# The expert weights of a mixture-of-experts stage in one contiguous piece per partition

## The chip, the cores and the metric

One core of a Trainium2 chip runs the whole program as one launch. The metric is the device time of that launch in microseconds (us). Before the change its median over three runs is 3550.05 us (3540.06 to 3554.87).

## The reference

The program computes two blocks on 512 tokens of 1024 features. The first is a convolution module and a retention module, the second is two layers of windowed attention with local mixers, each followed by a layer of routed experts. All is float32. The change touches only the routed experts and what feeds them. Cut to that:

```
# second block, per layer l (0: 512 + 256 context tokens, 1: 512 tokens)
hx = x * (1 + sc2) + sh2                       # modulated rows, 1024 features
y  = hier_moe(hx, w_rg, b_rg, w_re, b_re, w1, w3, w2)
x  = layer_norm(ALPHA * x + g2 * y, ln2_g, ln2_b)

def hier_moe(h, ...):
    g_logit = h @ w_rg + b_rg                  # 4 groups, the best one is taken
    e_logit = (h @ w_re + b_re) of that group  # 8 experts each, the best two
    gates   = p_group * softmax(best two)
    # per expert e, for its rows xb:
    ys = (silu(xb @ w1[e]) * (xb @ w3[e])) @ w2[e]    # w1, w3: 1024x512; w2: 512x1024
    return sum over a token's two experts of gate * ys
```

There are 32 experts in each of the two layers. The three matrices of one expert hold 2 MB each.

## The kernel before

**Stages.** The first block takes the span up to about 1350 us, then follow attention and mixers of layer 0, the experts of layer 0 (about 1680 to 2340 us), attention and mixers of layer 1, and the experts of layer 1 (about 2820 to 3500 us).

**What feeds the experts.** `modulated` on DVE (line 1415) writes `x * (1 + scale)` of 128 tokens to `b_hx`, and `add_shift` on POOL (line 1828) adds the shift in place. Both run for four sets of rows, q = 0 to 3: the even ones feed the attention of layer q/2, the odd ones the experts. For an odd q, ACT's DMA queue (line 787) writes the rows to `moe_in` in DRAM, and PE transposes them (line 968) and multiplies them with the router weights `b_wr` (line 1104). Feature k*128+p of a row stands on partition p as piece k, in the rows and in the router weights alike.

**The experts.** The rows of each expert are padded to blocks of 64. The 32 experts are shared out to two streams s = 0, 1 (the even and the odd ones), and the engines go round the streams: block i of stream 0, block i of stream 1, block i+1 of stream 0, and so on (`rounds`, line 366). Each stream has its own slots for w1, w3 and w2, its own rows and its own PSUM banks. A block is done like this:

- POOL gathers its 64 rows from `moe_in` with an indirect DMA (line 1888). Rows that are only padding are out of bounds and are left out.
- PE transposes them (line 1132), DVE copies them (1726), PE makes the two products with w1 and w3 (1145, 32 matmuls).
- ACT takes SiLU (805), DVE multiplies gate, SiLU and the other product into `m_h` (1752).
- PE transposes `m_h` (1156), DVE copies (1734), PE multiplies with w2 (1168, 16 matmuls), ACT (812) and DVE (1742) copy the result.
- POOL scatters the 64 rows to `moe_out` with an indirect DMA (line 1904).

PE's order in one step (`expert_step`, line 1173) is: products of block i, transposes of the hidden rows of block i-1, transposes of the rows of block i+1, outputs of block i-1; then the same for the other stream. POOL's order (`move_step`, line 1909) is: gather for block i+1, scatter of block i-1. So the scatter of one stream stands just ahead of the gather of the other in POOL's queue.

**The loads.** SP loads w1 and w3 of block i+1 when the products of block i are done, and w2 of block i when the outputs of block i-1 are done (`load_step`, line 565). `cond=new` leaves a load out where the block has the same expert as the one before it. In the tile `m_w` partition p holds, for each k, a row of 512 floats (w1, w3; k = 0 to 7) or of 1024 floats (w2; k = 0 to 3), and the row is row k*128+p of the matrix in DRAM:

```
ws = [a[k][l].rearrange("e (k p) n -> p (e k) n", p=P) for k in ("w1", "w3", "w2")]
sp.dma_start(m_w[s][j], ws[j][:, bass.ds(e * kk[j], kk[j]), :], cond=new)
```

A load therefore fills each partition from 8 separate stretches of 2 KB of DRAM (w1, w3) or from 4 of 4 KB (w2). All weights go through SP's DMA queue, gathers and scatters through POOL's queue; both share the core's 16 DMA engines.

Of the kernel before, what the change touches and what calls it, by code (L numbers as in the profile page):

```python
# [14 lines left out]
ALU = mybir.AluOpType  # L15
# [5 lines left out]
P = 128  # L21
D = 1024
KD = D // P
S = 512
C = 256
TX, TC = S // P, C // P
# [18 lines left out]
SB = 64  # L45
# [57 lines left out]
def build(nc, a, out, stop=None):  # L103
    ctx = ExitStack()
    with ctx:
# [9 lines left out]
        def mem(at, n, parts=P):  # L115
            return arena[0:parts, at:at + n]
# [45 lines left out]
        def ada_cols(v, g):  # L162
# [75 lines left out]
        m_si = [mem(W0 + 16800 + 8 * s, 1, SB).bitcast(I32) for s in range(2)]  # L238
        m_w = [[mem(RING + CHUNK * (3 * s + j), CHUNK).rearrange("p (k c) -> p k c", k=k)
                for j, k in enumerate((KD, KD, KE))] for s in range(2)]  # L240

# [189 lines left out]
        def _(sp):  # L431
# [85 lines left out]
            for l in range(LAYERS):  # L517
# [11 lines left out]
                for who in ((0, 1) if l == 0 else (0,)):  # L529
                    for i_, j in enumerate((2, 4, 3)):  # L530
                        mod_row(l, who, j, 3 * who + i_)
                sp.dma_start(b_wr, a["w_router"][l].rearrange("(k p) n -> p k n", p=P)).then_inc(sem("wr"), 16)
                sp.dma_start(mem(o_r, E * E), a["lower"]).then_inc(sem("wr"), 16)

                ws = [a[k][l].rearrange("e (k p) n -> p (e k) n", p=P) for k in ("w1", "w3", "w2")]
                kk = (KD, KD, KE)
                sp.wait_ge(sem("ob_mm"), past("ob_mm", l) + 2 * nt)
                for j, what in enumerate(("w1", "w3", "w2")):
                    sp.dma_start(m_w[0][j], ws[j][:, 0:kk[j], :]).then_inc(moe(l, 0, what), 16)

# [8 lines left out]
                for j, what in enumerate(("w1", "w3", "w2")):  # L549
                    sp.dma_start(m_w[1][j], ws[j][:, kk[j]:2 * kk[j], :]).then_inc(moe(l, 1, what), 16)  # L550
                sp.wait_ge(sem("meta"), past("meta", l) + 1)
                last = last_blocks(sp, l)

                def weights(s, j, what, e, new):

                    sp.dma_start(m_w[s][j], ws[j][:, bass.ds(e * kk[j], kk[j]), :], cond=new)\  # L556
                        .then_inc(moe(l, s, what), 16)
# [634 lines left out]
        def _(dve):  # L1192
# [170 lines left out]
            def finish_rows(q, tiles, first, mod_q, sc, free=None):  # L1363
# [22 lines left out]
                def mod_next(i_):  # L1386
                    dve.wait_ge(sem("row_x"), past_rows(q) + i_ + 1)
                    if mod_q % 2 == 0:
                        dve.wait_ge(sem("mod_in"), past("mod_in", mod_q // 2) + 64)
                    if free and tiles[i_] >= TX:  # L1390
                        free()
                    modulated(tiles[i_], sc)

# [20 lines left out]

            def modulated(t, sc):

                dve.scalar_tensor_tensor(out=b_hx[:, t, :], in0=b_mod[sc[t >= TX]], scalar=1.0, in1=xr[:, t, :],  # L1417
                                         op0=ALU.add, op1=ALU.mult).then_inc(sem("hx_scaled"), 1)
# [11 lines left out]
            for t in mod_order(0):  # L1430
                if t < TX:
                    dve.wait_ge(sem("fin_x"), t + 1)
                modulated(t, (3, 5))
            for i_ in range(T):
                mod_copy(0, i_)
            for l in range(LAYERS):
# [307 lines left out]
                def gate_step(s, i, early):  # L1744

                    if early >= 1:
# [4 lines left out]
                    dve.wait_ge(moe(l, s, "silu"), count(l, s, "silu", i + 1))  # L1751
                    dve.scalar_tensor_tensor(out=m_h[s], in0=m_sg[s], scalar=gate, in1=bank(4 * s)[0:SB],
                                             op0=ALU.mult, op1=ALU.mult).then_inc(moe(l, s, "hidden"), 1)
# [28 lines left out]
        def _(pool):  # L1782
# [45 lines left out]
            def add_shift(q, i_, sh):  # L1828
                t = mod_order(q)[i_]
                pool.wait_ge(sem("hx_scaled"), past("hx_in", q) + i_ + 1)  # L1830
                pool.tensor_tensor(b_hx[:, t, :], b_hx[:, t, :], b_mod[sh[t >= TX]], ALU.add)\  # L1831
                    .then_inc(sem("hx_in"), 1)
# [151 lines left out]
```

## Time and profile before

| | |
|---|---|
| median of 3 runs | 3550.05 us (3540.06 to 3554.87) |
| profiled execution, its time | 3556.9 us |
| its span | 3555.1 us |
| PE busy | 2875.6 us, 81% |
| DVE, ACT, POOL busy | 1172.8, 446.7, 416.5 us |
| mean granted clock | 0.88 |
| HBM read | 737.51 MB |

In the page a matmul's line is that of the kernel, DMA share is the mean busy share of the 16 DMA engines in a stretch, and GB/s what they moved. A granted clock of 1 is 2.4 GHz, 0.5 is 1.2 GHz.

### The profile page before, as it was taken

The page shows a single profiled execution, that of the slowest core. Times are in us where ns is not written, and L with a number is a line of the kernel's source. Part 1 is how long each engine was busy: PE and PEld are TensorE (multiplying, and loading weights), DVE is VectorE, ACT ScalarE, POOL GpSimd, SP SyncE. Part 2 cuts the span into 40 slices and gives each one's busy share as a digit, 9 for nine tenths or more (in the row PEclk, how much of TensorE's full clock was granted, in tenths as well). Part 3 has the DMA queues.
Part 4 walks back from the last instruction along what each step waited for, and adds up shares of the span by engine and source line. Part 5 has one row for each costly group of instructions (what it writes and reads, how often), then busy time and mean ns, then how long its engine had stood idle before and what let it go on. Part 6 is the DMA issues. An engine that isn't in the chain of part 4 may idle for free.

```text
span 3555.1 us, 33336 instructions
## 1 busy us (share of the span) xinstructions
PE 2875.6 (81%) x11308; PEld 1305.6 (37%) x11308; DVE 1172.8 (33%) x2041; ACT 446.7 (13%) x845; POOL 416.5 (12%) x488
## 2 busy tenths in 40 slices
PE   7999889999996996794888877818868488898872
PEld 3444334444443554443333222205434323333320
DVE  4899822300112214445111111164254411111114
ACT  2111131001100013400000000000141000000000
POOL 0110030000002000014111111122000311111111
PEclk9999999999998996795989898858879588998786
DMA  6666411221111210015768999751100597469992
GB/s 205 196 201 201 154 41 69 80 86 71 47 66 41 74 42 0 1 43 208 261 249 322 386 386 361 267 193 39 48 1 26 197 381 291 152 218 391 391 338 115
DMA packets 272120, 607.97 MB, mean 171 GB/s; under 512 B 18548, under 2 KB 43253, under 8 KB 270640
## 3 DMA queue, kind: packets, MB, share of 16 engines
q1 hardware_dynamic: 255216, 580.30, 45.1%
q0 software_dynamic: 15392, 21.47, 2.1%
q10 hardware_dynamic: 1440, 5.24, 0.4%
q8 instruction: 45, 0.74, 0.1%
q14 instruction: 27, 0.22, 0.0%
HBM read 737.51 MB, written 29.34 MB: 216 GB/s over the span
## 4 chain that ended last, share of the span: by engine, by line
PE 61%; DMA 13%; DVE 10%; issue 7%; ACT 3%; POOL 3%; SPq 2%; POOLq 1%; DVEq 0%; ACTq 0%
DMA arena<-moe_in,arena 10%; PE psum L1168 10%; PE psum L863 9%; PE psum L910 9%; PE psum L997 8%; PE psum L884 6%; PE psum L1089 4%; PE psum L1145 3%; SPq L556 2%; PE psum L1063 2%; PE psum L1132 2%; ACT arena L752 2%; PE psum L848 1%; DVE arena L1551 1%; DMA arena<-in_w 1%
## 5 line engine op out<-in xcount | busy, mean ns | idle before, releaser
L1145 PE MATMUL psum<-arena 128*64 128x512 f32 x2656 | 599.3, 604 | 35.7 <-DMA arena<-in_w 20.0
L1168 PE MATMUL psum<-arena 128*64 128x512 f32 x1328 | 404.6, 766 | 3.0 <-DVE arena L1734 2.6
L1145 PEld LDWEIGHTS psum<-arena 128*64 128x64 f32 x2656 | 196.3, 140 | 423.2 <-issue 422.8
L863 PE MATMUL psum<-arena 128*128 128x512 f32 x768 | 345.3, 603 | 2.9 <-ACT arena L625 2.9
L910 PE MATMUL psum<-arena 128*128 128x512 f32 x768 | 329.9, 592 | 0.8 <-ACT arena L617 0.8
L1244 DVE SCALAR_TENSOR_TENSOR arena<-arena 128x512 f32<-128x512 f32 x464 | 308.8, 747 | 0.0
L997 PE MATMUL psum<-arena 128*128 128x512 f32 (+1 forms) x800 | 284.5, 518 | 11.1 <-DMA arena<-in_w_in 10.2
L884 PE MATMUL psum<-arena 128*128 128x512 f32 x512 | 223.7, 600 | 11.1 <-POOL arena L1816 10.4
L1734 DVE COPY arena<-psum 128x256 f32<-128x256 f32 x83 | 35.3, 425 | 589.6 <-PE psum L1156 589.6
L1132 PE MATMUL psum<-arena 64*128 64x64 f32 x696 | 72.4, 259 | 179.0 <-DMA arena<-moe_in,arena 179.0
L910 PEld LDWEIGHTS psum<-arena 128*128 128x128 f32 x768 | 145.8, 190 | 184.2 <-issue 183.2
L863 PEld LDWEIGHTS psum<-arena 128*128 128x128 f32 x768 | 143.0, 191 | 174.9 <-issue 174.9
L997 PEld LDWEIGHTS psum<-arena 128*128 128x128 f32 x800 | 152.6, 191 | 142.1 <-issue 133.5
L1168 PEld LDWEIGHTS psum<-arena 128*64 128x64 f32 x1328 | 113.6, 174 | 230.2 <-issue 224.2
L1904 POOL DMA_INDIRECT moe_out<-arena x79 | 74.0, 937 | 1000.6 <-DVE arena L1742 1000.6
L1826 POOL TENSOR_TENSOR arena<-arena 128x1024 f32<-128x1024 f32 x20 | 58.6, 2931 | 858.7 <-DVE arena L1384 858.7
L1742 DVE COPY arena<-psum 64x512 f32<-64x512 f32 x83 | 57.5, 693 | 299.6 <-PE psum L1168 299.6
L884 PEld LDWEIGHTS psum<-arena 128*128 128x128 f32 x512 | 98.5, 193 | 135.9 <-issue 134.7
L1089 PE MATMUL psum<-arena 128*128 128x512 f32 x320 | 137.9, 593 | 1.7 <-ACT arena L769 1.7
L1831 POOL TENSOR_TENSOR arena<-arena 128x1024 f32<-128x1024 f32 x22 | 65.6, 2996 | 623.7 <-DVE arena L1417 623.7
L1726 DVE COPY arena<-psum 128x512 f32<-128x512 f32 x87 | 60.2, 692 | 236.3 <-PE psum L1132 235.6
L1132 PEld LDWEIGHTS psum<-arena 64*128 64x128 f32 x696 | 61.4, 167 | 190.1 <-issue 190.0
(253 smaller groups left out, 2352.2 us busy)
## 6 DMA issues: line engine op xcount, KB each, us to landing
arena<-in_w SPq DMA_DIRECT2D x257, 2048.0 KB
arena<-in_w_ada SPq DMA_DIRECT2D x48, 1024.0 KB, 5.2
arena<-in_conv_w_in SPq DMA_DIRECT2D x24, 1024.0 KB
arena<-in_ret_w_in SPq DMA_DIRECT2D x12, 2048.0 KB, 7.9
arena<-in_w_in SPq DMA_DIRECT2D x8, 2048.0 KB, 18.7
arena<-mod_rows SPq DMA_DIRECT2D x20, 512.0 KB, 8.5
arena<-moe_out SPq DMA_DIRECT2D x10, 1024.0 KB, 9.2
arena<-in_conv_w_out SPq DMA_DIRECT2D x4, 2048.0 KB, 10.2
```

The lines of the kernel that those rows point to most:

```text
L556: sp.dma_start(m_w[s][j], ws[j][:, bass.ds(e * kk[j], kk[j]), :], cond=new)\
L752: act.activation(sb, sb, ACT.Exp, bias=stats[:, o + 4 + hh:o + 5 + hh], accum_out=stats[:, o + 12 + hh:o + 13 + hh]).then_inc(sem("at_e"), 1)
L863: m = pe.matmul(bank(b + c), w[:, k, c * P:(c + 1) * P], c_hT[:, k, :], start=(k == 0), stop=(k == KD - 1))
L884: m = pe.matmul(bank(2 * t + hf), mem(y + S * k + P * t, P), slot_rows(n)[:, k % 4, hf * CW:(hf + 1) * CW], start=(k == 0), stop=(k == KI ...
L910: m = pe.matmul(bank(4 * (n % 2) + j), l_, r_, start=(k == 0), stop=(k == KD - 1))
L997: m = pe.matmul(o, l_, r_, start=(k == 0), stop=(k == KD - 1))
L1089: m = pe.matmul(bank(2 * (t % 4) + hf), y[:, t * P:(t + 1) * P], slot_rows(base + 4 + k // 4)[:, k % 4, hf * CW:(hf + 1) * CW], start=(k = ...
L1132: m = pe.transpose(bank(4 * s + 1, SB, SB * k), m_xs[s][:, k * P:(k + 1) * P], ident[0:SB, 0:SB])
L1145: m = pe.matmul(bank(4 * s)[part], m_xsT[s][:, k, :], m_w[s][j][:, k, :], start=(k == 0), stop=(k == KD - 1))
L1168: m = pe.matmul(bank(4 * s + 3)[SB * hf:SB * hf + SB], m_hT[s][:, k, :], m_w[s][2][:, k, hf * CW:(hf + 1) * CW], start=(k == 0), stop=(k = ...
L1244: ins = dve.scalar_tensor_tensor(out=acc, in0=u, scalar=w[:, j:j + 1], in1=acc, op0=ALU.mult, op1=ALU.add)
L1904: pool.indirect_dma_start(out=moe_out[l], in_=m_y[s], in_offset=None, out_offset=bass.IndirectOffsetOnAxis(m_si[s], 0), bounds_check=2 * n ...
```

## The change

The three weight matrices are read so that partition p takes rows p*8 to p*8+7 (w1, w3) or p*4 to p*4+3 (w2) of the matrix. In DRAM these rows are neighbours, so each partition's share is one stretch of 16 KB. The slot in SBUF keeps its layout: piece k of partition p is now feature p*8+k (w1, w3) or hidden feature p*4+k (w2).

The other operand of each product has to follow. PE still transposes columns k*128 to k*128+127 of a row, so feature p*8+k has to stand in column k*128+p: `modulated` and `add_shift` write the rows in that order where they feed the experts (odd q), and the product with gate writes `m_h` likewise with 4 in place of 8. The router weights are read in the same feature order, which makes one stretch of 1152 bytes per partition of eight of 144 bytes.

No engine gets or loses a compute instruction, and their order stays. SP issues the same DMAs in the same order with other shapes. On DVE and POOL the odd-q instructions get the shape 128x128x8 in place of 128x1024 with a step of 512 bytes between neighbours in SBUF; for even q both sides stay contiguous.

```diff
-        m_w = [[mem(RING + CHUNK * (3 * s + j), CHUNK).rearrange("p (k c) -> p k c", k=k)
-                for j, k in enumerate((KD, KD, KE))] for s in range(2)]
+        m_slot = [[mem(RING + CHUNK * (3 * s + j), CHUNK) for j in range(3)] for s in range(2)]
+        m_w = [[m_slot[s][j].rearrange("p (k c) -> p k c", k=k) for j, k in enumerate((KD, KD, KE))]
+               for s in range(2)]
+        def feature_order(v):
+            return v.rearrange("p (f k) -> p f k", k=KD)
+        def hx_out(q, t):
+            return b_hx[:, t, :].rearrange("p (f k) -> p f k" if q % 2 == 0 else "p (k f) -> p f k", k=KD)
...
-                sp.dma_start(b_wr, a["w_router"][l].rearrange("(k p) n -> p k n", p=P)).then_inc(sem("wr"), 16)
+                sp.dma_start(b_wr, a["w_router"][l].rearrange("(p k) n -> p k n", p=P)).then_inc(sem("wr"), 16)
...
-                ws = [a[k][l].rearrange("e (k p) n -> p (e k) n", p=P) for k in ("w1", "w3", "w2")]
+                ws = [a[k][l].rearrange("e (p k) n -> p e (k n)", p=P) for k in ("w1", "w3", "w2")]
...
-                    sp.dma_start(m_w[s][j], ws[j][:, bass.ds(e * kk[j], kk[j]), :], cond=new)\
+                    sp.dma_start(m_slot[s][j].unsqueeze(1), ws[j][:, bass.ds(e, 1), :], cond=new)\
                         .then_inc(moe(l, s, what), 16)
...
-                dve.scalar_tensor_tensor(out=b_hx[:, t, :], in0=b_mod[sc[t >= TX]], scalar=1.0, in1=xr[:, t, :],
+                dve.scalar_tensor_tensor(out=hx_out(q, t), in0=feature_order(b_mod[sc[t >= TX]]), scalar=1.0,
+                                         in1=feature_order(xr[:, t, :]),
                                          op0=ALU.add, op1=ALU.mult).then_inc(sem("hx_scaled"), 1)
...
-                    dve.scalar_tensor_tensor(out=m_h[s], in0=m_sg[s], scalar=gate, in1=bank(4 * s)[0:SB],
+                    dve.scalar_tensor_tensor(out=m_h[s].rearrange("t (k f) -> t f k", k=KE),
+                                             in0=m_sg[s].rearrange("t (f k) -> t f k", k=KE), scalar=gate,
+                                             in1=bank(4 * s)[0:SB].rearrange("t (f k) -> t f k", k=KE),
                                              op0=ALU.mult, op1=ALU.mult).then_inc(moe(l, s, "hidden"), 1)
...
-                pool.tensor_tensor(b_hx[:, t, :], b_hx[:, t, :], b_mod[sh[t >= TX]], ALU.add)\
+                pool.tensor_tensor(hx_out(q, t), hx_out(q, t), feature_order(b_mod[sh[t >= TX]]), ALU.add)\
                     .then_inc(sem("hx_in"), 1)
```

## Rows read from the trace of the kernel before

**Rows 1.** The page: span in 40 slices, PE and DMA, then GB/s.

```profile
PE   7999889999996996794888877818868488898872
DMA  6666411221111210015768999751100597469992
GB/s 205 196 201 201 154 41 69 80 86 71 47 66 41 74 42 0 1 43 208 261 249 322 386 386 361 267 193 39 48 1 26 197 381 291 152 218 391 391 338 115
```

**Rows 2.** Waits in 1650 to 2500 us, then 2820 to 3500: us, times, longest.

```profile
PE psum L1132 <- DMA arena<-moe_in,arena: 90.8, 32, 7.1
PE psum L1145 <- DMA arena<-in_w: 13.5, 4, 5.2
...
PE psum L1132 <- DMA arena<-moe_in,arena: 88.1, 37, 5.3
PE psum L1145 <- DMA arena<-in_w: 6.5, 1, 6.5
```

**Rows 3.** The source view of line 1145: PE idle until the weights landed, us, times.

```profile
  DMA arena<-in_w: 20.0, 5
```

**Rows 4.** Timeline near 3400 us: start, us, engine line, tiles, [idle before].

```profile
3393.88 7.03 PE L1145 MATMUL psum<-arena 128*64 128x512 f32 x32
...
3395.78 0.93 POOL L1904 DMA_INDIRECT moe_out<-arena  x1 [13.86 <-DVE arena L1742]
...
3397.75 0.96 POOL L1888 DMA_INDIRECT arena<-moe_in,arena  x1 [0.85 <-POOL arena L1885]
...
3404.80 1.08 PE L1132 MATMUL psum<-arena 64*128 64x64 f32 x8 [3.51 <-DMA arena<-moe_in,arena]
3405.82 5.70 PE L1168 MATMUL psum<-arena 128*64 128x512 f32 x16
...
3411.35 0.59 PE L1145 MATMUL psum<-arena 128*64 128x512 f32 x2
```

**Rows 5.** Timeline near 3095 us, and the next block.

```profile
3091.09 7.03 PE L1145 MATMUL psum<-arena 128*64 128x512 f32 x32
...
3094.95 0.95 POOL L1888 DMA_INDIRECT arena<-moe_in,arena  x1 [0.85 <-POOL arena L1885]
...
3098.68 0.68 PE L1132 MATMUL psum<-arena 64*128 64x64 f32 x8 [0.17 <-DMA arena<-moe_in,arena]
3099.29 3.65 PE L1168 MATMUL psum<-arena 128*64 128x512 f32 x16
...
3102.78 0.60 PE L1145 MATMUL psum<-arena 128*64 128x512 f32 x2
```

**Rows 6.** Windows: us, busy by engine, clock, DMA share, GB/s.

```profile
425.00:437.00 12.00, 0.00 (x0) 0.00 (x0) 10.42 (x16) 0.00 (x0) 1.47 (x2) 0.57 1.01 411
2346.00:2358.00 12.00, 0.00 (x0) 0.00 (x0) 10.90 (x16) 0.35 (x2) 0.00 (x0) 0.50 1.01 425
2364.00:2376.00 12.00, 0.00 (x0) 0.00 (x0) 11.72 (x12) 0.20 (x1) 6.18 (x2) 0.50 1.05 391
```

**Rows 7.** The page's DMA issues: KB each, us from issue to landing.

```profile
arena<-in_ret_w_in SPq DMA_DIRECT2D x12, 2048.0 KB, 7.9
```

**Rows 8.** Timeline near 1850 us, after a block that loads nothing.

```profile
1836.71 1.88 PE L1145 MATMUL psum<-arena 128*64 128x512 f32 x8
...
1843.64 7.04 PE L1145 MATMUL psum<-arena 128*64 128x512 f32 x32
...
1845.53 0.93 POOL L1904 DMA_INDIRECT moe_out<-arena  x1 [9.01 <-DVE arena L1742]
...
1847.61 0.96 POOL L1888 DMA_INDIRECT arena<-moe_in,arena  x1 [0.95 <-POOL arena L1885]
...
1854.10 1.09 PE L1132 MATMUL psum<-arena 64*128 64x64 f32 x8 [3.03 <-DMA arena<-moe_in,arena]
```

**Rows 9.** Groups by line and shape: DVE and POOL, busy us, mean ns.

```profile
L1752 DVE SCALAR_TENSOR_TENSOR arena<-arena,psum 64x512 f32<-64x512 f32 x83 | 60.6, 730 | 0.0
L1831 POOL TENSOR_TENSOR arena<-arena 128x1024 f32<-128x1024 f32 x22 | 65.6, 2996 | 623.7 <-DVE arena L1417 623.7
```

**Rows 10.** Timeline of the rows for the experts of layer 1.

```profile
2772.77 5.57 POOL L1831 TENSOR_TENSOR arena<-arena 128x1024 f32<-128x1024 f32 x2 [1.16 <-DVE arena L1417]
...
2776.08 1.97 PE L968 MATMUL psum<-arena 128*128 128x128 f32 x8 [2.71 <-POOL arena L1831]
```

More of the change, by code:

```diff
@@ L531, in _ @@
                         mod_row(l, who, j, 3 * who + i_)
-                sp.dma_start(b_wr, a["w_router"][l].rearrange("(k p) n -> p k n", p=P)).then_inc(sem("wr"), 16)
+                sp.dma_start(b_wr, a["w_router"][l].rearrange("(p k) n -> p k n", p=P)).then_inc(sem("wr"), 16)
                 sp.dma_start(mem(o_r, E * E), a["lower"]).then_inc(sem("wr"), 16)
-                ws = [a[k][l].rearrange("e (k p) n -> p (e k) n", p=P) for k in ("w1", "w3", "w2")]
-                kk = (KD, KD, KE)
+                ws = [a[k][l].rearrange("e (p k) n -> p e (k n)", p=P) for k in ("w1", "w3", "w2")]
                 sp.wait_ge(sem("ob_mm"), past("ob_mm", l) + 2 * nt)
                 for j, what in enumerate(("w1", "w3", "w2")):
-                    sp.dma_start(m_w[0][j], ws[j][:, 0:kk[j], :]).then_inc(moe(l, 0, what), 16)
+                    sp.dma_start(m_slot[0][j], ws[j][:, 0, :]).then_inc(moe(l, 0, what), 16)
                 sp.wait_ge(sem("hx_in"), past("hx_in", 2 * l + 1) + nt)
@@ L549, in _ @@
                 for j, what in enumerate(("w1", "w3", "w2")):
-                    sp.dma_start(m_w[1][j], ws[j][:, kk[j]:2 * kk[j], :]).then_inc(moe(l, 1, what), 16)
+                    sp.dma_start(m_slot[1][j], ws[j][:, 1, :]).then_inc(moe(l, 1, what), 16)
                 sp.wait_ge(sem("meta"), past("meta", l) + 1)
@@ L1391, in mod_next @@
                         free()
-                    modulated(tiles[i_], sc)
+                    modulated(mod_q, tiles[i_], sc)
                 dve.wait_ge(sem("row_w"), 32 * (q + 1))
@@ L1413, in finish_rows, with modulated @@
                     mod_copy(mod_q, i_)
-            def modulated(t, sc):
-                dve.scalar_tensor_tensor(out=b_hx[:, t, :], in0=b_mod[sc[t >= TX]], scalar=1.0, in1=xr[:, t, :],
+            def modulated(q, t, sc):
+                dve.scalar_tensor_tensor(out=hx_out(q, t), in0=feature_order(b_mod[sc[t >= TX]]), scalar=1.0,
+                                         in1=feature_order(xr[:, t, :]),
                                          op0=ALU.add, op1=ALU.mult).then_inc(sem("hx_scaled"), 1)
@@ L1432, in _ @@
                     dve.wait_ge(sem("fin_x"), t + 1)
-                modulated(t, (3, 5))
+                modulated(0, t, (3, 5))
             for i_ in range(T):
```

## The prediction

> **What bounds the kernel now.** I read the page's 40 slices first, then the waits of PE in the two stages of the experts, then the timeline of single blocks, and last short windows in which only one kind of transfer runs.
>
> In the slices [rows 1] DMA counts only where the experts run. Slices are 89 us. Slices 19 to 26 and 32 to 39 are the experts' stages, and in five of them the rate is 381 to 391 GB/s with a DMA share of 9 tenths or more (1955 to 2133 us, 2844 to 2933 us, 3200 to 3377 us). PE is busy 7 or 8 tenths there. Neither engine is plainly the bound, so the waits must tell.
>
> PE waits for the weights themselves hardly at all: 13.5 us in layer 0 and 6.5 us in layer 1 [rows 2], five waits in all, 20.0 us [rows 3]. It waits for the gathered rows 32 times in layer 0 (90.8 us) and 37 times in layer 1 (88.1 us) [rows 2]. So the transfer that holds PE is the small gather of 64 rows on POOL's queue, not the 6 MB of weights.
>
> Two blocks show what the gather costs. Near 3400 us, with the DMA engines full, the gather is issued at 3397.75 and PE's transposes start at 3404.80, 7.05 us later, after PE has idled 3.51 us; from one set of products to the next it is 3411.35 - 3393.88 = 17.47 us [rows 4]. Near 3095 us the same gather takes 3098.68 - 3094.95 = 3.73 us, PE idles 0.17 us, and the block lasts 3102.78 - 3091.09 = 11.69 us [rows 5]. Of the 5.78 us between them 3.34 are the idle time; another 2.05 are in the 16 output matmuls, 5.70 us against 3.65 [rows 4, 5], which run partly at the lower clock after PE has idled. So each block is a ring: outputs, DVE copy, scatter, gather, transposes, outputs of the other stream. The weights' transfers lengthen the ring through the gather.
>
> **The change part by part.**
>
> *Weights in 16 KB pieces.* The trace has no 16 KB piece of this queue, so I take its cost from three full windows [rows 6]. The 2 KB pieces of in_w_in go at 391 GB/s, the 4 KB pieces of conv_w_out at 411, the 8 KB pieces of moe_out at 425. One of 16 engines thus takes 2048 B / 24.4 GB/s = 84 ns, 159 ns and 308 ns for a piece. From 4 to 8 KB that is 74.4 ns for each further 2 KB, so 16 KB should take 308 + 4 x 74.4 = 606 ns, an estimate. A load of 128 pieces is 8 for each engine: 4.85 us, against 64 x 84 ns = 5.36 us (w1, w3) and 32 x 159 ns = 5.10 us (w2). An expert comes to 14.55 us after 15.82, 1.27 us or 8% less. For 64 experts that is 81 us of DMA time. The bounds: none of it is worth anything where the ring sets the pace, all of it where DMA does.
>
> Where does it meet PE? First in the five direct waits [rows 3], of which I let half go: -10 us (0 to -20). Second in the ring. In a 17.5 us block w1 and w3 are issued when the products end (3400.9) and the next scatter follows at about 3413.2, 12.3 us later. The page gives 7.9 us from issue to landing for 2 MB in 2 KB pieces [rows 7], 2.5 us above the 5.36 of transfer; 2 x 4.85 + 2.5 = 12.2 us are then through. Only w2, issued when the outputs end, stands before scatter and gather. It ends 5.10 - 4.85 = 0.25 us sooner. For 64 loading blocks that is -16 us. The ends: 0 if the gather passes w2 anyway, and -1.27 us for each block, -81 us, if DMA sets the pace; between them I stay near the ring, since the waits [rows 2] put 179 us on the gather and 20 on the weights.
>
> *What the long pieces do to the small ones.* Scatter and gather bring 64 rows each, 4 rows and one completion count for each engine: 10 small packets. Behind a queue of 2 KB pieces and one of 4 KB pieces the gather takes about the same, 6.49 us [rows 8] and 7.05 us [rows 4]. If every small packet lets one weight piece pass, it waits 10 x 84 ns = 0.8 us today and 10 x 606 ns = 6.1 us then, 5.2 us more, provided at least 10 pieces are queued for each engine. In the ordinary block they aren't: w2 has 8 pieces, some of them done. After a block that loads nothing they are: near 1845 us the outputs follow the products so soon that the scatter goes out at 1845.53, 7 us after w1 and w3 could be issued (products end at 1836.71 + 1.88 = 1838.59 [rows 8]); of their 12.2 us 5.2 are left, some 8 pieces, and the 8 of w2 stand behind them. There are 83 blocks (instances of line 1752 [rows 9]) and 64 experts, so 19 blocks load nothing; about ten of them are followed by one that does. With 1.3 us each, a quarter of the full price because the queue that delays the gather is empty afterwards and the next gather goes free, this is +13 us (0 to +52).
>
> The Trainium skill says in "DMA: Bandwidth & Descriptors", section on queues, rings and completion order, that a DMA engine goes round its queues at packet granularity and drains a whole packet before it switches. That the two [rows 4, 8] are nearly equal neither supports nor excludes it, since both kinds of piece are short; by that rule the 5.2 us are real wherever the queue is deep. This is the rule that speaks against the change, and the second rival below is built on the same mechanism.
>
> *Strided writes.* DVE's product with the gate takes 730 ns [rows 9]. It writes each element 512 B from the last; the trace has no such write. Even doubled it is done in 1.5 us beside the outputs' 3.65 us or more, with DVE free until these end. Cost 0; without the cover 0.73 us x 83 = 61 us. The router's rows are written by DVE and then added to by POOL, 10 times each. In layer 0 POOL keeps ahead of PE, which is busy with the previous tile's router products. In layer 1 PE waits 2.71 us for POOL's shift, of which two take 5.57 us [rows 10]. Bounds: 0, or twice as long, +5.6 us; I take the middle, +3 us, as DVE's write goes with it.
>
> "GPSIMD Engine Reference" of the Trainium skill, in its performance pitfalls, puts an SBUF read with a step over 8 bytes at 2.9 cycles an element in place of 1.9. By this the two instructions would cost 2.8 us more; no row here has such a step.
>
> *Router weights.* 128 longer pieces in place of 1024 short ones, loaded while PE is at the output projection. Cost 0.
>
> **The sum.** -10 - 16 + 13 + 3 = -10 us on the profiled execution's 3556.9 us: 3546.9. The median stands 7 us below that execution, so I predict 3540 us.
>
> **The rivals.**
>
> *Faster: DMA sets the pace.* For it speak the five slices at 381 to 391 GB/s and the five waits for weights. Against it speak 179 us of waits for rows beside 20 for weights. If half of the 81 us come back, with a share of blocks in which PE's idle time gets so short that the outputs run in 3.65 us and not 5.70 (say 5 x 2 us), it is -50: 3500 us. All of it and more such blocks would be 3460.
>
> *Slower: the gather behind long pieces.* One mechanism, at the gather of a loading block, from the point where 10 pieces (6 us of transfer) are queued for each engine. Its full price is 5.2 us a block. Against it: the longer the gather waits, the further the queue empties, so it can't hit every block. If it takes 1.3 us on the mean in 64 blocks instead of in 10, it is +83 - 13 = +70 beside the sum: 3610 us. At a third of that, 3565.
>
> *It doesn't do what it says.* The pieces are split on the way, or DRAM gives no more for 16 KB than for 4 KB. Then only the strided writes are left: 3550 to 3556 us. Against it speaks the growth up to 8 KB [rows 6].
>
> **How the numbers follow.** A run of this kernel can tell about 0.5%, 17.8 us, from no change, so faster means below 3532 and slower above 3568. My forecast has 0.32, the rival that nothing happens 0.06; both lie within the bound: same 0.38. DMA as the bound has 0.36: faster 0.36. The gather behind long pieces has 0.26: slower 0.26. The likeliest case alone is 3525 to 3560. The range for 8 in 10 takes in most of both rivals: 3490 to 3600.
>
> **What will show it.** (1) Full windows of the experts' stage read 425 to 432 GB/s; at 391 the first term is wrong. (2) The waits of line 1132 for the gathered rows: near 165 us in all for my forecast, below 120 for the first rival, above 230 for the second; and a loading block after an idle one has its transposes 8 us or more after the gather is issued. (3) Line 1145's waits for weights fall to about 10 us. (4) The gate product stays under 1.5 us and nobody waits for it; line 1831's rows for the experts take 2.8 to 5.6 us. (5) Everything before 1500 us is unchanged. The forecast fails if the gathers' waits move by more than 50 us either way.

## The result, and the profile after the change

| | before | after |
|---|---|---|
| median, same chip | 3552.46 us (3540.06 to 3568.31, 20 runs) | 3566.94 us (3551.12 to 3576.74, 20 runs) |
| ratio of the times | 1 | 1.0032, 95% interval 1.0017 to 1.0048 |
| profiled execution, span | 3555.1 us | 3559.2 us |
| DMA packets | 272120 | 131064 |

The change makes the kernel slower by 0.32%, 11 us. The forecast was 3540 us, 10 us faster than the 3550.05 us it started from. The time lies in the range, the direction is wrong.

A single execution of either kernel lies up to 16 us from its median, and the two profiled ones are 4.1 us apart. So sizes below come from ratios, and the profiles show where waits are; each profile is one execution. All lines of PE and ACT are 8 higher after the change: 1132 is now 1140, 1145 is 1153, 1156 is 1164, 1168 is 1176. DVE's 1752 is 1761, POOL's 1831 is 1842, the gather is 1899, the scatter 1915.

The page after the change: 40 slices, then q1 (the weights' queue), then PE's groups with busy time, mean ns and idle time before them.

```profile
DMA  6566411221111200015668998651100497459982
GB/s 210 190 201 201 154 48 62 94 71 71 47 66 52 80 25 0 1 43 208 263 265 326 386 393 336 261 193 39 48 1 26 185 374 274 182 200 392 388 360 118
...
q1 hardware_dynamic: 114160, 580.30, 42.6%
...
L1153 PE MATMUL psum<-arena 128*64 128x512 f32 x2656 | 592.9, 599 | 12.9 <-DMA arena<-in_w 7.4
L1176 PE MATMUL psum<-arena 128*64 128x512 f32 x1328 | 387.8, 738 | 2.2 <-DVE arena L1743 1.8
...
L1140 PE MATMUL psum<-arena 64*128 64x64 f32 x696 | 72.7, 259 | 229.5 <-DMA arena<-moe_in,arena 229.5
```

The same page of before has q1 at 45.1% of the span. 45.1% of 3555.1 us is 1603 us and 42.6% of 3559.2 us is 1516 us: the weights take 87 us less of DMA time. The pieces themselves are as fast as forecast: in the packet records of the trace after the change a piece of 16384 bytes takes 611 ns (median; 606 was estimated), and there are 24576 of them, 128 for each of 192 loads, so none is split. In the trace before, pieces of 2048 and 4096 bytes take 84 to 86 and 159 to 160 ns.

None of the 87 us is left at the end. The five slices with 381 to 391 GB/s [rows 1] read 374 to 393 now; DMA stands idle in the gained time. That shows in a window over the loop of layer 0: us, busy by engine, clock, DMA share, GB/s. First before, then after.

```profile
1700.00:2330.00 630.00, 505.86 (x2334) 184.87 (x2332) 96.42 (x158) 45.70 (x77) 87.57 (x152) 0.88 0.88 318
```

```profile
1700.00:2330.00 630.00, 495.54 (x2318) 180.16 (x2314) 109.83 (x156) 45.67 (x77) 87.39 (x151) 0.88 0.81 318
```

The DMA share falls from 0.88 to 0.81 at the same 318 GB/s. PE's waits after the change, in 1650 to 2500 us and then in 2820 to 3500 us, answer to [rows 2]:

```profile
PE psum L1140 <- DMA arena<-moe_in,arena: 129.0, 36, 7.6
...
PE psum L1140 <- DMA arena<-moe_in,arena: 100.5, 38, 7.1
PE psum L1153 <- DMA arena<-in_w: 7.4, 1, 7.4
```

The waits for weights fall from 20.0 to 7.4 us, those for the gathered rows rise from 179.0 [rows 2, 90.8 + 88.1] to 229.5. The timeline after the change near 2015 us shows two blocks in a row, to be held against [rows 4]:

```profile
2001.80 7.04 PE L1153 MATMUL psum<-arena 128*64 128x512 f32 x32
2003.68 0.94 POOL L1915 DMA_INDIRECT moe_out<-arena  x1 [13.87 <-DVE arena L1751]
...
2005.78 0.97 POOL L1899 DMA_INDIRECT arena<-moe_in,arena  x1 [0.95 <-POOL arena L1896]
...
2015.88 1.09 PE L1140 MATMUL psum<-arena 64*128 64x64 f32 x8 [6.65 <-DMA arena<-moe_in,arena]
2016.89 5.81 PE L1176 MATMUL psum<-arena 128*64 128x512 f32 x16
2022.54 7.03 PE L1153 MATMUL psum<-arena 128*64 128x512 f32 x32
...
2026.31 0.96 POOL L1899 DMA_INDIRECT arena<-moe_in,arena  x1 [0.85 <-POOL arena L1896]
...
2031.28 0.69 PE L1140 MATMUL psum<-arena 64*128 64x64 f32 x8 [1.32 <-DMA arena<-moe_in,arena]
2031.89 3.65 PE L1176 MATMUL psum<-arena 128*64 128x512 f32 x16
```

From the first gather's issue to the transposes it takes 2015.88 - 2005.78 = 10.10 us, from the second's 4.97 us. Before it was 7.05 us in [rows 4], and 7.22, 6.41 and 6.17 us in the three blocks from 2004 to 2044 us. Counting transposes that start after 4.5 us or more of idle time in the whole timeline gives 3 before (17.8 us in all) and 23 after (135.1 us).

The DMA issues of a window with full queues, 1960 to 2050 us, show how long the small transfers take. The last number is the median of us from issue to landing. First before, then after.

```profile
moe_out<-arena POOLq DMA_INDIRECT x5, 5.6
arena<-moe_in,arena POOLq DMA_INDIRECT x5, 6.0
```

```profile
moe_out<-arena POOLq DMA_INDIRECT x5, 8.8
arena<-moe_in,arena POOLq DMA_INDIRECT x5, 7.2
```

The scatter, first of the two in POOL's queue, takes 3.2 us longer (2.6 in the window from 3200 to 3370 us: 8.2 after 5.6). Its 5 packets for each engine at 606 - 84 to 606 - 159 ns, the prediction's piece times, are 2.2 to 2.6 us.

The typical gather is no slower, only some are much slower. Over all 87 gathers the median from issue to landing goes from 5.9 to 5.4 us and the mean from 5.5 to 5.9; those over 8 us go from 1 to 21.

The packet records also say how many pieces pass. Take a scatter and the gather behind it: 160 small packets, 10 for each engine. From the first to the last of them, 0.34 pieces of 16 KB start for each small packet at the median of layer 0 (0.18 in layer 1), and 0.93 (0.96) or more in the highest tenth of such pairs. That stretch lasts 4.2 us on the mean (3.5 in layer 1), and 7.3 (6.1) or more in its longest tenth; before it was 3.5 (3.2) and 4.7 (3.8). So one piece for each small packet is what the worst blocks come near, not the rule. With short pieces the median is 2.1 (2.5), more than one for one.

### The profile page after: what moved, and what is told of

The parts are those of the page before. It is cut to its first block, busy times and chain, and to the rows that moved or that the text cites. A ratio compares the mean times of both kernels' runs of the same rounds, so it can differ in the third digit from the quotient of the medians.

```text
span 3559.2 us, 33336 instructions
## 1 busy us (share of the span) xinstructions
PE 2851.0 (80%) x11308; PEld 1297.9 (36%) x11308; DVE 1210.4 (34%) x2041; ACT 446.7 (13%) x845; POOL 426.1 (12%) x488
## 2 busy tenths in 40 slices
DMA packets 131064, 607.97 MB, mean 171 GB/s; under 512 B 16500, under 2 KB 41461, under 8 KB 105008
## 3 DMA queue, kind: packets, MB, share of 16 engines
q1 hardware_dynamic: 114160, 580.30, 42.6%
## 4 chain that ended last, share of the span: by engine, by line
PE 61%; DMA 14%; DVE 10%; issue 7%; POOL 3%; ACT 3%; POOLq 1%; SPq 0%; DVEq 0%; ACTq 0%
DMA arena<-moe_in,arena 13%; PE psum L1176 11%; PE psum L871 9%; PE psum L918 9%; PE psum L1005 8%; PE psum L892 6%; PE psum L1097 4%; PE psum L1153 3%; PE psum L1140 2%; ACT arena L760 2%; PE psum L1071 2%; DVE arena L1751 1%; PE psum L856 1%; DVE arena L1560 1%; PE psum L939 1%
## 5 line engine op out<-in xcount | busy, mean ns | idle before, releaser
L1153 PE MATMUL psum<-arena 128*64 128x512 f32 x2656 | 592.9, 599 | 12.9 <-DMA arena<-in_w 7.4
L1176 PE MATMUL psum<-arena 128*64 128x512 f32 x1328 | 387.8, 738 | 2.2 <-DVE arena L1743 1.8
L1153 PEld LDWEIGHTS psum<-arena 128*64 128x64 f32 x2656 | 192.7, 139 | 396.3 <-issue 395.9
L1140 PE MATMUL psum<-arena 64*128 64x64 f32 x696 | 72.7, 259 | 229.5 <-DMA arena<-moe_in,arena 229.5
L1176 PEld LDWEIGHTS psum<-arena 128*64 128x64 f32 x1328 | 109.2, 169 | 216.8 <-issue 210.5
L1837 POOL TENSOR_TENSOR arena<-arena 128x1024 f32<-128x1024 f32 x20 | 62.1, 3107 | 852.2 <-DVE arena L1392 852.2
L1842 POOL TENSOR_TENSOR arena<-arena 128x1024 f32<-128x1024 f32 x22 | 71.7, 3274 | 626.2 <-DVE arena L1425 626.2
```

What stands on the lines that cost most here:

```text
L1140: m = pe.transpose(bank(4 * s + 1, SB, SB * k), m_xs[s][:, k * P:(k + 1) * P], ident[0:SB, 0:SB])
L1153: m = pe.matmul(bank(4 * s)[part], m_xsT[s][:, k, :], m_w[s][j][:, k, :], start=(k == 0), stop=(k == KD - 1))
L1176: m = pe.matmul(bank(4 * s + 3)[SB * hf:SB * hf + SB], m_hT[s][:, k, :], m_w[s][2][:, k, hf * CW:(hf + 1) * CW], start=(k == 0), stop=(k = ...
L1842: pool.tensor_tensor(hx_out(q, t), hx_out(q, t), feature_order(b_mod[sh[t >= TX]]), ALU.add)\
```

## Experiments

The edits are shown shortened. The two columns of waits are PE's idle time in one profiled execution of each run, before the transposes of gathered rows and before the products.

Theory: small packets of scatter and gather take turns with the pieces of the weights, so long pieces hold the gather up, and PE waits for the gather. Rival: the strided writes cost the time.

| run | ratio to before (95% interval) | waits for rows, us | waits for weights, us |
|---|---|---|---|
| before | 1 | 179.0 | 20.0 |
| after | 1.0032 (1.0017 to 1.0048) | 229.5 | 7.4 |
| e1 short pieces | 1.0000 (0.9984 to 1.0016) | 148.2 | 61.5 |
| e2 strided reads | 1.0062 (1.0039 to 1.0085) | 206.7 | 6.7 |
| e3 w2 in 4 KB | 0.9993 (0.9976 to 1.0009) | 197.5 | 5.1 |
| e9 w2 in 8 KB | 1.0018 (1.0002 to 1.0034) | 218.1 | 6.4 |
| e4 only w2 in 16 KB | 1.0068 (1.0042 to 1.0093) | 240.2 | 9.3 |
| e12 late w2, after | 1.0200 (1.0173 to 1.0228) | 269.5 | 7.2 |
| e15 late w2, before | 0.9990 (0.9971 to 1.0009) | 128.7 | 83.4 |
| e5 early gather, before | 0.9808 (0.9784 to 0.9833) | 14.5 | 124.4 |
| e6 early gather, after | 0.9642 (0.9617 to 0.9667) | 14.5 | 98.5 |
| e10 gather first, before | 0.9875 (0.9849 to 0.9902) | 55.1 | 116.6 |
| e11 gather first, after | 0.9804 (0.9777 to 0.9832) | 130.3 | 37.3 |
| e13 early, w2 in 4 KB | 0.9669 (0.9645 to 0.9692) | 14.7 | 111.7 |
| e16 early, short pieces | 0.9811 (0.9787 to 0.9836) | 14.7 | 134.3 |
| e7 no loads, before | 0.9145 (0.9119 to 0.9171) | 25.6 | 0 |
| e8 no loads, after | 0.9153 (0.9125 to 0.9180) | 25.4 | 0 |

### Pieces against strided writes (e1, e2)

e1 keeps the change's feature order and writes but loads 2 KB and 4 KB pieces:

```diff
-sp.dma_start(m_slot[s][j].unsqueeze(1), ws[j][:, bass.ds(e, 1), :], cond=new)
+sp.dma_start(m_w[s][j][:, ::-1, :].unsqueeze(1),
+             ws[j].rearrange("p e (k n) -> p e k n", k=k)[:, bass.ds(e, 1), :, :], cond=new)
...
-m_w[s][j][:, k, :]
+m_w[s][j][:, KD - 1 - k, :]
```

> The kernel after the change, with its strided writes and its feature order, but each load of weights again in 8 pieces of 2 KB (w1, w3) or 4 pieces of 4 KB (w2): the pieces go to the slot in reverse order, so that none can be joined to the next. Theory (long pieces hold up the gather): the waits for gathered rows fall from 229.5 us back to 175 to 190, the direct waits for weights rise from 7.4 to about 20, and the time is before plus the 2 to 3 us of the router's rows, ratio 0.999 to 1.002. Rival (the strided writes cost the time): the gate product still takes 1.09 us, the waits for rows stay near 230, and as the gain of the long pieces is lost too, the ratio is 1.003 to 1.007.

3553.15 us, the time of before. This run differs from the one after the change in the pieces alone, and the two intervals (up to 1.0016, from 1.0017) don't overlap: the long pieces cost the time. The strided writes and the feature order by themselves cost at most 0.16%, while the gate product takes 1099 ns in this run too. No gather takes over 8 us. Where the waits lie differs from the theory: 148.2 us for rows and 61.5 for weights in place of 179 and 20. Their sum, 209.7, is near the 199.0 of before. Why they shift is open.

e2 is the other half: all rows written plainly, PE's transposes read with a step.

```diff
-b_hx[:, t, k * P:(k + 1) * P], ident)
+b_hx[:, t, k * P:(k + 1) * P] if q % 2 == 0 else b_hx[:, t, k::KD], ident)
...
-m_xs[s][:, k * P:(k + 1) * P],
+m_xs[s][:, k::KD],
...
-m_h[s][:, k * P:(k + 1) * P],
+m_h[s][:, k::KE],
```

> The kernel after the change with its 16 KB pieces, but all rows are written in plain order, and TensorE's transposes read every 8th (rows, router) or every 4th (hidden rows) column instead. Theory (long pieces hold up the gather): the waits for rows stay at 215 to 240 us, the time is the one after the change less the 2 to 3 us of the router's rows, ratio 1.001 to 1.004, unless the strided transposes themselves take longer than the 259 ns of after. Rival (the strided writes cost the time): the gate product is back at 0.73 us, the waits for rows fall below 190, the ratio is 0.995 to 0.999.

3575.4 us, slower than the change itself, although DVE's and POOL's times are those of before (730 ns for the gate product). The transposes of the hidden rows, after the change and in e2 (mean ns is the second number behind the bar):

```profile
L1164 PE MATMUL psum<-arena 64*128 64x64 f32 x332 | 38.4, 239 | 23.7 <-issue 23.7
```

```profile
L1164 PE MATMUL psum<-arena 64*128 64x64 f32 x332 | 56.9, 294 | 23.7 <-issue 23.7
```

They cost 18.5 us more of PE, and PE is 40.2 us busier in all (2891.2 after 2851.0). So e2 cannot price the strided writes from the other side. It does show 206.7 us of waits for rows with plain writes, against 179.0, and 18 gathers over 8 us: the rival doesn't have these. Yet 206.7 is also below the 215 to 240 expected. Whether PE's longer transposes cover part of the waits isn't shown.

### Which load's pieces (e3, e4, e9)

e3 has 4 KB pieces for w2 and 16 KB pieces for the rest; e4 the reverse. The part that follows (gate product or modulated rows) goes with each.

```diff
+short = (2,)          # e3; e4 has (0, 1)
-ws = [a[k][l].rearrange("e (p k) n -> p e (k n)", p=P) for k in ("w1", "w3", "w2")]
+ws = [a[k][l].rearrange("e (k p) n -> p (e k) n" if j in short else "e (p k) n -> p e (k n)", p=P)
+      for j, k in enumerate(("w1", "w3", "w2"))]
```

> w1 and w3 in 16 KB pieces, w2 in 4 KB pieces as before the change, and with it the gate product writes plain rows. Theory in its first form (the pieces of w2, issued just ahead of scatter and gather, hold the gather up): waits for rows 175 to 195 us, direct waits for weights near 8, ratio 0.995 to 0.999. In its second form (what is left of w1 and w3 in the queues holds it up): waits for rows 215 to 240, ratio 1.001 to 1.004. Rival (the strided gate product costs the time): as the first form, but the next experiment then is as the first form too.

> w2 in 16 KB pieces, w1 and w3 in 2 KB pieces as before the change, rows for the experts and router in plain order, the gate product strided. Theory in its first form (w2's pieces hold the gather up): waits for rows 215 to 240 us, ratio 1.001 to 1.005. In its second form (w1 and w3): waits for rows 175 to 195 us, ratio 0.998 to 1.001. Rival (the strided gate product): ratio 1.002 to 1.005, at waits for rows of 215 to 240 that the experiment before, which has a plain gate product, does not show.

e9 has the change with w2 in two 8 KB pieces:

```diff
-sp.dma_start(m_slot[s][j].unsqueeze(1), ws[j][:, bass.ds(e, 1), :], cond=new)
+in_ = in_.rearrange("p o (h c) -> p o h c", h=2)                       # w2 only
+sp.dma_start(in_slot(s, j).unsqueeze(1), in_, cond=new)                # halves in reverse order
...
-m_w[s][2][:, k, hf * CW:(hf + 1) * CW],
+m_w[s][2][:, (k + 2) % 4, hf * CW:(hf + 1) * CW],
```

> The kernel after the change with w2 in two pieces of 8 KB (halves of a partition's share, in reverse order in the slot); w1 and w3 stay in 16 KB pieces, all strided writes stay. Theory (each small packet of scatter and gather lets one piece of w2 pass): about half of the way from 16 KB back to 4 KB, waits for rows 205 to 222 us, ratio 1.000 to 1.002. Rival (the piece's size doesn't matter, contiguous reading as such does): waits for rows 225 to 235, ratio 1.003 to 1.004.

With w1 and w3 long, w2 in 4, 8 and 16 KB pieces gives ratios of 0.9993, 1.0018 and 1.0032, waits for rows of 197.5, 218.1 and 229.5 us, 6, 13 and 23 waits of 4.5 us or more, and 3, 11 and 21 gathers over 8 us. The ratios of neighbours overlap in their intervals, those of the ends don't. From before, w2 alone in 16 KB pieces (e4) costs 0.68%, 24 us. So in this order of issue w2's long pieces are the whole loss, the first form of the theory. e3's 197.5 us and 0.9993 lie just outside what that form expected, and e4's 1.0068 above its 1.005. That w1's and w3's long pieces give a little back (1.0068 to 1.0032) is likely but not shown, since the intervals meet. That the strided gate product takes part here is excluded only through e1; e9 and the change both have it and still differ in their waits.

### The queue before the gather (e12, e15)

In the first 16 blocks of each stream w2's load waits until the other stream's next gather has landed:

```diff
 sp.wait_ge(moe(l, s, "out"), count(l, s, "out", i))
+if early == 3:
+    sp.wait_ge(moe(l, 1 - s, "gather"), count(l, 1 - s, "gather", 16 * (i + s) + 32))
 weights(s, 2, "w2", e, new)
```

> The kernel after the change; in the first 16 blocks of each stream SP issues w2's load only when the other stream's next gather has landed, so that no piece of w2 stands ahead of it. Theory (w2's pieces hold the gather up): waits for rows fall from 229 us below 120, and although w2 then starts 6 to 8 us later, the time falls to 3460 to 3540 us. Rival (what is left of w1 and w3 holds it up): waits for rows stay above 200 us and the time rises above 3575.

My theory said under 120 us of waits and a faster kernel; it is 269.5 us and 2.0% slower. The rival of that expectation has its way. The timeline of e12 (its lines: products 1164, transposes 1151, scatter 1926, gather 1910):

```profile
1965.06 0.97 POOL L1910 DMA_INDIRECT arena<-moe_in,arena  x1 [0.85 <-POOL arena L1907]
...
1969.17 0.69 PE L1151 MATMUL psum<-arena 64*128 64x64 f32 x8 [0.46 <-DMA arena<-moe_in,arena]
...
1973.27 7.04 PE L1164 MATMUL psum<-arena 128*64 128x512 f32 x32
...
1977.24 0.96 POOL L1910 DMA_INDIRECT arena<-moe_in,arena  x1 [0.95 <-issue]
...
1985.96 1.08 PE L1151 MATMUL psum<-arena 64*128 64x64 f32 x8 [5.27 <-DMA arena<-moe_in,arena]
```

One gather is there after 4.11 us, the next takes 8.72 us. The first row below is SP's queue in the same timeline: from 1969.31 us, when the first gather has landed, SP issues loads of weights again.

```profile
1969.31 38.51 SPq L564 DMA_DIRECT2D arena<-in_w  x9
```

SP issues in the order of its program, so the delayed w2 also delays the w1 and w3 behind it: the trace has w2's issue at 1969.31, w1's at 1971.60 and w3's at 1972.02, up to 14.55 us of transfer by the prediction's estimate. The next gather comes at 1977.24. By its semaphore w2 has landed at 1976.7, w1 lands at 1981.7 and w3 at 1987.0, and SP issues the next w2 only at 1986.10. So w1's and w3's pieces alone stand beside this gather, and 148 of them start between the first and the last of the 160 small packets. It isn't w2 as such: it is any long piece that is still queued when the small packets come.

The same edit of the kernel before:

> The kernel before the change with the edit of late w2: in the first 16 blocks of each stream SP issues w2's load only when the other stream's next gather has landed. Theory (long pieces hold up small packets whichever load they belong to; loading late itself costs little): at most 1.0% slower than before, 3540 to 3585 us, waits for rows 170 to 210 us, and a gather in a full window lands below 6.5 us. Rival (loading w2 late is what costs, with pieces of any size): 2% slower as with long pieces, 3610 to 3630 us.

3550.21 us and gathers that land in 6.1 us in the window from 1960 to 2050 us, as the theory had it. Its waits for rows, 128.7 us, are well below the 170 to 210 expected and again turned into waits for weights. Loading w2 late costs nothing with short pieces and 2% with long ones.

### The gather off PE's path (e5, e6, e13, e16)

POOL issues the other stream's next gather ahead of each scatter, one block sooner. The order in the loop, before and with the edit:

```diff
-gather(0, i + 1)  scatter(0, i - 1)  gather(1, i + 1)  scatter(1, i - 1)
+gather(1, i + 1)  scatter(0, i - 1)  gather(0, i + 2)  scatter(1, i - 1)
```

> The kernel before the change; only POOL's order differs: the gather of the other stream's next rows is issued ahead of each scatter, not behind it, so it goes out about half a round (one block) sooner. Theory (PE's pace is a ring through scatter, gather and transposes; a load of one expert takes 15.8 us of DMA, so a block that loads lasts about 17 us by DMA alone): the waits for rows fall from 179 us below 40, but most comes back as waits for weights, and the time is 3500 to 3550 us. Rival (the gather's wait is PE's loss alone and DMA has room): 3400 to 3450 us, waits for weights below 60.

> The kernel after the change with the same earlier gathers. Theory: long pieces hurt only through the gather that PE waits for; with the gather early the 8% shorter loads count: waits for rows below 40 us, 3440 to 3500 us, ratio to the same edit of the kernel before 0.975 to 0.99. Rival (long pieces delay everything, or the strided writes cost): no faster than the same edit of the kernel before, ratio 1.00 to 1.005.

3483.93 and 3425.21 us. Both are faster than their theory said (3500 to 3550 and 3440 to 3500): e5 lies between its theory and its rival, and its 124.4 us of waits for weights show that DMA has not as much room as the rival needs. e6's ratio to e5, 0.983, is as expected. The waits for rows are down to 14.5 us in both, and now the change is worth 3483.93 - 3425.21 = 59 us, 1.7%. The landing of the gathers didn't improve, in 1960 to 2050 us they take 6.2 us in e5 and 9.5 in e6; PE no longer waits for them. The DMA slices of e6:

```profile
DMA  6666312122201210012488999951100469659992
GB/s 205 200 209 198 133 76 89 68 81 74 74 0 68 89 50 25 1 45 104 146 350 347 412 411 384 385 202 40 49 0 27 191 264 367 236 189 423 425 379 100
```

They reach 412 and 425 GB/s where the highest of before are 386 and 391 [rows 1]. e6 takes 3.6% less than the kernel before and, by the ratios, 3.9% less than the kernel after the change.

e13 is e3 with early gathers, e16 is e1 with early gathers; the edits are those shown above. Both times lie in the range of their theory and outside that of the rival.

> Early gathers, w1 and w3 in 16 KB pieces, w2 in 4 KB pieces with a plain gate product. Theory (once the gather is early PE waits for weights alone, and every shorter load counts): w2's 0.25 us for each of 64 experts are lost against early gathers with all pieces long (3425 us): 3430 to 3445 us. Rival (w2's long pieces still hold something up that PE waits for): 3405 to 3420 us, faster than all long.

> Early gathers in the layout after the change, with strided writes, but all weights in 2 KB and 4 KB pieces (in reverse order in the slot). Theory (the gain of early gathers with long pieces over early gathers with short ones is the pieces' faster transfer, and strided writes cost 2 to 4 us): 3484 to 3492 us, as early gathers in the layout before (3484) plus these. Rival (the contiguous share of each partition, in whatever pieces, makes the reading faster): 3425 to 3450 us.

3437.44 us: w2's long pieces, which cost 14 us with the late gather (e3 to the change, 0.39%), gain about 10 us with the early one (0.9669 to 0.9642, 0.27%; the intervals still touch). 3486.09 us: in the layout after the change, short pieces give the time of e5. The gain of e6 is the length of the pieces; the strided writes cost 0.03% beside it, less than the intervals can tell.

### The place in POOL's queue (e10, e11)

As e5 and e6, but the gather may go no sooner than the scatter did (first 15 blocks of each stream):

```diff
+pool.wait_ge(moe(l, 0, "y"), count(l, 0, "y", 2 * i))
...
 gather(1, i + 1, 3)
 scatter(0, i - 1, 1)
+pool.wait_ge(moe(l, 1, "y"), count(l, 1, "y", 2 * i))
...
 gather(0, i + 2, 3)
```

> The kernel before the change; the next gather is issued ahead of the scatter but no sooner than the scatter was (it waits for the same copied result; only in the first 15 blocks of each stream, later ones go as early as they can). It goes out 2 us sooner than before, with 5 small packets of its own to each engine and none of the scatter's ahead. In a full window (1960 to 2050 us) the gather lands 5.2 to 6.0 us after its issue (5.9 to 6.0 before). Both theories: waits for rows fall to 80 to 120 us, 3495 to 3530 us.

> The same edit of the kernel after the change. Theory (each small packet lets one piece pass, 606 ns for 16 KB): the gather now takes the scatter's place in the line and the scatter's landing time, 8.0 to 9.0 us in a full window, 2.5 to 3.5 us more than the same edit of the kernel before; the time is 3450 to 3500 us. Rival (only the bytes ahead count, not the pieces' size): it lands within 0.5 us of the same edit of the kernel before.

Landings in 1960 to 2050 us, e10 and then e11:

```profile
arena<-moe_in,arena POOLq DMA_INDIRECT x5, 6.2
```

```profile
arena<-moe_in,arena POOLq DMA_INDIRECT x5, 8.4
```

The gather takes 2.2 us longer behind long pieces (2.6 in 3200 to 3370 us, 8.7 after 6.1); 2.5 to 3.5 was expected for the first window. e10's own 6.2 us is above the 5.2 to 6.0 expected, so taking the scatter's packets from in front of it gained nothing there. e11 at 3483.17 us lies in the range; e10 at 3504.32 too, with fewer waits for rows (55.1 us) than the 80 to 120 expected.

### The ring alone (e7, e8)

The loads inside the loop are left out; every block uses its stream's first expert.

```diff
-sp.dma_start(..., cond=new).then_inc(moe(l, s, what), 16)
+sp.sem_inc(moe(l, s, what), 16)
```

> The kernel before the change without the loads of weights inside the experts' loop (each stream computes all blocks with its first expert's weights). This is the ring with empty queues. Both theories: waits for rows below 25 us, a block 11 to 12 us, 83 blocks about 970 us in place of 1306, so 3190 to 3260 us.

> The kernel after the change without the loads inside the loop. Theory (strided writes are hidden in the experts' stages): 2 to 5 us longer than the same edit of the kernel before, all of it at the router's rows. Rival (the strided gate product, 0.36 us longer, costs in each of 83 blocks): 25 to 35 us longer.

3248.0 and 3251.75 us, both times as expected. The timeline of e7 (its products are line 1144, its transposes 1131, its outputs 1167):

```profile
2903.16 7.04 PE L1144 MATMUL psum<-arena 128*64 128x512 f32 x32
...
2907.01 0.96 POOL L1887 DMA_INDIRECT arena<-moe_in,arena  x1 [0.85 <-POOL arena L1884]
...
2910.60 0.68 PE L1131 MATMUL psum<-arena 64*128 64x64 f32 x8
2911.27 3.65 PE L1167 MATMUL psum<-arena 128*64 128x512 f32 x16
2914.75 7.04 PE L1144 MATMUL psum<-arena 128*64 128x512 f32 x32
```

With empty queues a block lasts 11.59 us with no wait for rows; the 302 us from here to 3550.22, the time of before beside it, are what the loads cost through both kinds of wait and the clock. Between e7 and e8, by medians, the strided writes cost 3.75 us (the runs overlap), not the 30 us by which the gate products got longer, and the waits for rows are the same.

## Why the prediction was wrong, step by step

The step that failed is the ring in the ordinary block. The prediction gave it -16 us through a w2 that is through sooner, and priced the gather behind long pieces for ten blocks only, +13 us: -3 together. The waits for rows rose by 50.5 us instead, and w2's long pieces cost 14 to 24 us of the kernel's time.

- **The direct waits, -10 us.** Right: 20.0 to 7.4 us, -12.6.
- **w2 is through 0.25 us sooner, -16 us.** Wrong in sign; this step and the next failed together. The prediction took w2 as a stretch of transfer that stands before scatter and gather as a whole. The runs show that w2 in 16 KB pieces costs 14 us (e3 to the change) to 24 us (before to e4) as long as PE waits for the gather.
- **Long pieces and small packets, +13 us.** The mechanism was right, and its full price of 5.2 us for 10 packets fits the 2.2 to 3.2 us measured for 5; the prediction's "every small packet lets one weight piece pass" holds only near the worst blocks (0.93 to 0.96 pieces), and not for the short pieces of before. Its reach was wrong. The prediction excluded the ordinary block because w2 has only 8 pieces for each engine and the price was worked out for 10, and so counted ten blocks. But 8 pieces are nearly the whole price, and 5 packets are half of it. The timeline near 2015 us shows it in an ordinary block. Waits of 4.5 us or more went from 3 to 23, the waits for rows from 179.0 to 229.5 us: +50.5 where -3 was forecast (-16 and +13). In the next block the gather goes free (4.97 us), as the prediction said.
- **What took most of it back.** PE's other times in the experts' stages fell: the outputs' busy time from 404.6 to 387.8 us and the products' from 599.3 to 592.9 by the two pages, and the idle time before the products by 22.8 (35.7 to 12.9, the direct waits among it). Together -46.0 us against +50.5, which fits the 4.1 us between the two profiled executions; the 11 us between the medians are more than these two profiles show. That the shorter busy times come from short waits, after which the outputs run in 3.65 us, is read from the timeline and not tested by itself.
- **The pieces' transfer, -1.27 us for an expert.** Right: 611 ns for a piece, and 87 us less in all, 81 forecast. It went into idle DMA. For that reason the sign given for it failed: the fullest slices of the kernel after the change read 386 to 393 GB/s, not 425 to 432, and 391 was to mean that this term is wrong. With the gather early (e6) they read 411 to 425.
- **Strided writes.** The gate product takes 1095 ns (under 1.5 us was said), and the 23.7 us of idle time before the transposes of its result are the same in both kernels: hidden. The router's rows, after the change, answer to [rows 10]:

```profile
2781.90 7.08 POOL L1842 TENSOR_TENSOR arena<-arena 128x1024 f32<-128x1024 f32 x2 [1.86 <-DVE arena L1425]
...
2786.22 1.97 PE L976 MATMUL psum<-arena 128*128 128x128 f32 x8 [4.40 <-POOL arena L1842]
```

  Two shifts take 7.08 us after 5.57, and PE waits 4.40 after 2.71, and 1.08 longer for the shift before that: 2.8 us, where +3 was forecast. The add reads and writes the rows in place with a step of 512 B, and takes 3.30 us in place of 2.79, 2.86 in place of 2.35 and 4.27 in place of 3.25: 0.5 to 1.0 us more. The 2.8 us more for two shifts, by the Trainium skill's "GPSIMD Engine Reference" (performance pitfalls), are not borne out: it is 1.51.
- **The rivals.** The slower one, gather behind long pieces, is what happened, at the foot of its range: 3565 us was given for a third of its price, and the median is 3566.94. The faster one (DMA sets the pace) is refuted for this kernel and is right for e6, where PE waits 98.5 us for weights and 14.5 for rows. The third, that the pieces are split on the way or come no faster, is refuted by the 611 ns.
- **The signs.** The prediction said above 230 us of waits for rows for the slower rival; it is 229.5. It was to fail if these waits moved by more than 50 us; they moved by 50.5. Its 165 us for the forecast itself doesn't follow from its terms, since 179 - 16 + 13 is 176.

The Trainium skill's rule in "DMA: Bandwidth & Descriptors" (queues, rings and completion order), a whole packet is drained before the engine goes on to the next queue, agrees with the landings above, 8.8 after 5.6 us and 8.4 after 6.2, if one piece of 16 KB is taken for a packet. The 2.1 to 2.5 short pieces for each small packet don't fit one piece to a turn; how pieces make packets, no run here shows. The prediction quoted it as the rule against the change and then gave it ten blocks.

What stays open: why in e1 and e15 waits for rows turn into waits for weights at the same time, and why layer 0 bears the loss. By the two profiles its last outputs start 7.8 us later (2335.77 after 2328.00), while layer 1 regains 5.0 (from its first transposes to its last outputs 656.55 us after 661.55).

## What to carry to other kernels

Before making a bulk transfer's pieces longer, look for a small transfer on another queue of the same DMA engines that something waits for: as an estimate for the worst case its delay is the number of its packets (with those ahead in its own queue) times the growth of the piece, up to the pieces queued. Here the worst tenth came near that, and most blocks stayed far below it. Count a shorter transfer as a gain only where the waits name that transfer. And do the two edits in the right order: first take the small transfer off the path by issuing it earlier (here 1.9% by itself), then lengthen the pieces (here 1.7% more, where alone it cost 0.3%).

## What was unexpected of the hardware

- A mean or a median can hide such a delay: the median gather got faster (5.9 to 5.4 us), while 21 of 87 in place of 1 took over 8 us and PE waited 50.5 us more.
- Moving work off the queue in front of a gather doesn't help if it lands in front of the next one: late w2 costs nothing in 2 and 4 KB pieces (0.9990) and 2% in 16 KB pieces (1.0200).
- TensorE's transposes are slower when they read columns 16 B apart: 294 ns mean in place of 239 for the hidden rows. DVE's product with a write step of 512 B takes 1095 ns in place of 730.
- An engine's strided writes can slow another engine's plain work: POOL's add of line 1837, unchanged, takes 3.82 to 3.87 us in place of 3.25 to 3.27 in six of the eight instances that run beside DVE's strided write of line 1425; the other two stay at 2.34 to 2.35. In e2, with plain writes, the six are at 3.25 to 3.27 again.
- In 1960 to 2050 us, with small transfers between them, pieces of 2 and 4 KB give 387 GB/s, and 385 where they go to SBUF in reverse order (e1); 16 KB pieces give 412 (e6).
